# Two-layer YOCO trunk on one core: the first squares, the keys' low half, the last PLE product and the first weights are placed earlier, and ScalarE issues the transfers of layer one's key squares

## What is computed

```
q, k, v, z = split(x @ w_in_a, 4)                 # layer one: 2048 x 8192
z_scores = q k^T / sqrt(128);  past = key < query
log_1m = where(past, log_sigmoid(-z_scores), 0)
tail = reversed cumsum(log_1m) - log_1m
w = where(past, exp(log_sigmoid(z_scores) + tail), 0)
y = (w v  *  silu(z)) @ w_out_a
x = LayerNorm(alpha * x + y, ln_g, ln_b)
x = x + (p[i] @ w_ple[i]) * sigmoid(x @ w_ple_gate[i])
# shared K/V = split(LayerNorm(x) @ w_kv), K rotated; layer two:
q, z = split(x @ w_in_b, 2);  y = (softmax(rope(q) K^T) V * silu(z)) @ w_out_b
# then the same LayerNorm and the same PLE gate, whose result is the output
```

## Time and profile before

| | |
|---|---|
| median of 3 runs | 1149.44 us (1148.65 to 1149.66) |
| the profiled execution | 1152.77 us |
| its span, first to last instruction | 1151.1 us |
| busy: TensorE matmul, weight load | 1139.9 us (99%), 951.0 us (83%) |
| busy: VectorE, ScalarE, GpSimd | 745.8 us (65%), 590.9 us (51%), 232.6 us (20%) |
| chain that ended last, by engine | TensorE 91%, DMA 3%, VectorE, GpSimd, ScalarE, issue and SyncE 1% each |

### The profile page before, as it was taken

One profiled execution on the slowest core, in us unless ns is written; L12 is line 12 of the kernel. 1 busy time (PEld: TensorE's weight loads), 2 busy tenths in 40 slices (PEclk: granted clock), 3 DMA queues, 4 the chain that ended last, 5 costly groups with the idle time before them and its releaser, 6 DMA issues.

```text
span 1151.1 us, 15530 instructions
## 1 busy us (share of the span) xinstructions
PE 1139.9 (99%) x5274; PEld 951.0 (83%) x5274; DVE 745.8 (65%) x795; ACT 590.9 (51%) x669; POOL 232.6 (20%) x475
## 2 busy tenths in 40 slices
PE   9989999999999999999999999999999999999998
PEld 8878888888888888888888888888888888888887
DVE  6646556556465657578888785456776676656873
ACT  6555557446556453546454555555554545334641
POOL 1222320340232300002536753420000010000000
PEclk9999999999999999999999999999999999999999
DMA  9866775675676686457787876774555575763571
GB/s 305 270 208 178 208 217 151 195 228 171 185 209 178 199 311 217 148 164 256 228 275 228 246 243 215 226 218 149 183 161 183 159 243 162 258 199 117 190 239 70
DMA packets 126587, 235.67 MB, mean 205 GB/s; under 512 B 13856, under 2 KB 16160, under 8 KB 126032
## 3 DMA queue, kind: packets, MB, share of 16 engines
q1 hardware_dynamic: 110176, 209.74, 59.0%
q0 software_dynamic: 16368, 25.37, 6.8%
HBM read 216.71 MB, written 4.19 MB: 192 GB/s over the span
## 4 chain that ended last, share of the span: by engine, by line
PE 91%; DMA 3%; DVE 1%; POOL 1%; ACT 1%; issue 1%; SPq 1%; DVEq 0%; ACTq 0%
PE acc L1189 28%; PE acc L1191 28%; PE acc L1190 28%; DMA raw<-in_w_in_a 3%; PE aux L1223 2%; POOL heads L430 1%; PE aux L1216 1%; ACT w_hi L480 1%; DMA heads<-big 1%; PE aux L1249 1%; PE aux L1263 1%; DVE w_lo L749 1%; PE aux L1394 0%; PE aux L1238 0%; PE aux L1191 0%
## 5 line engine op out<-in xcount | busy, mean ns | idle before, releaser
L749 DVE TENSOR_TENSOR w_lo<-raw,w_hi 128x1024 fp32r<-128x1024 f32 x388 | 470.1, 1222 | 344.9 <-ACT w_hi L480 344.6
L480 ACT ACTIVATE w_hi<-raw 128x1024 fp32r<-128x1024 f32 x388 | 408.9, 1058 | 441.7 <-PE acc L1191 360.3
L1189 PE MATMUL acc<-w_hi,act 128*128 128x512 f32 x1548 | 608.0, 393 | 0.1
L1191 PE MATMUL acc<-w_hi,act 128*128 128x512 f32 x1548 | 603.1, 390 | 0.0
L1190 PE MATMUL acc<-w_lo,act 128*128 128x512 f32 x1548 | 602.6, 389 | 0.0
L1191 PEld LDWEIGHTS acc<-w_hi,act 128*128 128x128 f32 x1548 | 290.7, 188 | 61.4
L1189 PEld LDWEIGHTS acc<-w_hi,act 128*128 128x128 f32 x1548 | 290.9, 188 | 59.4 <-issue 0.7
L1190 PEld LDWEIGHTS acc<-w_lo,act 128*128 128x128 f32 x1548 | 291.0, 188 | 58.8
L430 POOL DMA_DIRECT2D heads<-big x192 | 93.8, 497 | 281.9 <-DVE big L770 238.1
L430 POOL DMA_DIRECT2D heads<-v_or_z x64 | 31.2, 496 | 52.0 <-DVE v_or_z L770 39.1
L430 POOL DMA_DIRECT2D stage<-v_or_z x48 | 23.5, 499 | 69.5 <-DVE v_or_z L988 43.7
(11 more groups left out here) (158 smaller groups left out, 653.2 us busy)
## 6 DMA issues: line engine op xcount, KB each, us to landing
raw<-in_w_in_a SPq DMA_DIRECT2D x124, 512.0 KB, 3.9
raw<-in_w_ple_gate SPq DMA_DIRECT2D x64, 512.0 KB, 4.8
raw<-in_w_in_b SPq DMA_DIRECT2D x64, 512.0 KB, 4.6
raw<-in_w_kv SPq DMA_DIRECT2D x64, 512.0 KB, 3.9
raw<-in_w_out_a SPq DMA_DIRECT2D x32, 512.0 KB, 4.5
raw<-in_w_out_b SPq DMA_DIRECT2D x32, 512.0 KB, 4.8
heads<-big POOLq DMA_DIRECT2D x192, 32.0 KB, 3.4
heads<-in_ln_rows POOLq DMA_DIRECT2D x4, 1024.0 KB, 7.9
```

What stands on the lines that cost most here:

```text
L480: nc.scalar.activation(w_hi[:, r], raw[:, r % RAWS], ACT.Copy).then_inc(hi_ready, 1)
L749: nc.vector.tensor_tensor(w_lo[:, r], raw[:, r % RAWS], w_hi[:, r].bitcast(F32), ALU.subtract) \
L1189: nc.tensor.matmul(dst, hi, w_hi[:, r, i], start=begin, stop=False)
L1191: mm = nc.tensor.matmul(dst, lo, w_hi[:, r, i], start=False, stop=end)
```

## The change

`WARM_UPS` is 12. The first two half pieces of weights are issued by ScalarE, ahead of its first instruction, and SyncE leaves them out. VectorE turns the first Q chunk after split 2 of its stretch (before: 3) and the first K chunk after split 3 (before: 6), ahead of `queries_lo(0)`. In all four groups `keys_lo` stands ahead of split 5. The key squares of all four groups are moved by 16 transfers that ScalarE issues after split 0 of the V chunk, with the same wait for `chunk_evac`; GpSimd keeps those of Q and Z. The tile 0 part of the last PLE product stands between the two token tiles of the last gate piece.

```
--- before.py
+++ after.py
@@ -34,7 +34,7 @@
 PIECE_K = 2
 RAWS = 4
 SPLITS = 8
-WARM_UPS = 14
+WARM_UPS = 12
 SQUARE = 32
 MOVED = 16 * (P // SQUARE) ** 2
 
@@ -335,7 +335,8 @@
                 for i, (x_sem, w_sem) in enumerate(((x_half_landed[j], w_half_landed[j]), (x_landed[j], w_landed[j]))):
                     rows = slice((j * PIECE_K + i) * P, (j * PIECE_K + i + 1) * P)
                     sp.dma_start(x_raw[:, PIECE_K * j + i], xt[rows, :]).then_inc(x_sem, 16)
-                    sp.dma_start(raw[:, j, i], wa[rows, 0:COLS]).then_inc(w_sem, 16)
+                    if j > 0:
+                        sp.dma_start(raw[:, j, i], wa[rows, 0:COLS]).then_inc(w_sem, 16)
             for j in range(RAWS, PC):
                 sp.dma_start(x_raw[:, PIECE_K * j:PIECE_K * (j + 1), :],
                              xt[j * PIECE_K * P:(j + 1) * PIECE_K * P, :].rearrange("(k p) t -> p k t", p=P)) \
@@ -433,7 +434,6 @@
 
             for g in range(G):
                 exchange(chunk_evac, g * 4 + 1, qT_flat, qn, q_moved)
-                exchange(chunk_evac, g * 4 + 2, kT_flat, kn, k_moved)
                 exchange(chunk_evac, g * 4 + 4, gt_flat, zn, z_moved)
             pool.wait_ge(pv_done, 2 * G)
             load_res(0, x)
@@ -586,6 +586,8 @@
                 nc.scalar.activation(w1_parts[:, 0, b], s[:, :, 0:T], ACT.Copy).then_inc(weights_hi, 1)
 
 
+            for i, w_sem in enumerate((w_half_landed[0], w_landed[0])):
+                act.dma_start(raw[:, 0, i], w_in_a[0][i * P:(i + 1) * P, 0:COLS]).then_inc(w_sem, 16)
             for j in range(RAWS):
                 for i, (x_sem, w_sem, x_done, w_done) in enumerate((
                         (x_half_landed[j], w_half_landed[j], x_half_hi, w_half_hi),
@@ -606,11 +608,23 @@
             nc.scalar.activation(neg_ones[:, :], neg_ones_raw, ACT.Copy).then_inc(masks_done, 1)
 
 
+            def exchange(turned, count, dst, src, moved):
+
+                act.wait_ge(turned, count)
+                for a in range(NS):
+                    for g in range(NS):
+                        act.dma_start(dst[g * SQUARE:(g + 1) * SQUARE, a * HT // NS:(a + 1) * HT // NS],
+                                      src[a * SQUARE:(a + 1) * SQUARE, g * HT // NS:(g + 1) * HT // NS]) \
+                            .then_inc(moved, 16)
+
+            def move_k(k):
+                exchange(chunk_evac, k * 4 + 2, kT_flat, kn, k_moved)
+
             def after_k(k):
                 return {5: [lambda: q_copies(k)]}
 
             def after_v(k):
-                return {4: [lambda: k_copies(k)], 6: [lambda: exp_abs(k, 0)],
+                return {0: [lambda: move_k(k)], 4: [lambda: k_copies(k)], 6: [lambda: exp_abs(k, 0)],
                         7: [lambda: values_hi(k), lambda: exp_abs(k, 1), lambda: log_1p(k)]}
 
             def after_z(k):
@@ -854,8 +868,7 @@
                 return {6: [lambda: queries_lo(k)]} | squares_end(n, 1, kn)
 
             def v_steps(k, n):
-                return {5: [lambda: keys_lo(k)],
-                        7: [lambda: values_lo(k), lambda: evacuate_v(n, 0, vn_a), lambda: softplus(k, 0)]}
+                return {7: [lambda: values_lo(k), lambda: evacuate_v(n, 0, vn_a), lambda: softplus(k, 0)]}
 
             def evacuate_v(n, parity, dst):
 
@@ -872,16 +885,16 @@
                 return {5: [lambda: gate_group(k, k, sz_a)], 6: [lambda: gated_lo(k, k, k + S_OUT[0])]}
 
             dve.wait_ge(consts_done, 12)
-            pieces(0, 0, {3: [lambda: turn_squares(PC, 0, qn)]})
-            pieces(PC, 0, {4: [lambda: queries_lo(0)], 6: [lambda: turn_squares(2 * PC, 1, kn)]})
+            pieces(0, 0, {2: [lambda: turn_squares(PC, 0, qn)]})
+            pieces(PC, 0, {3: [lambda: turn_squares(2 * PC, 1, kn)], 4: [lambda: queries_lo(0)]})
             with dve.Fori(0, G - 1) as g:
                 n = g * (4 * PC) + 2 * PC
-                pieces(n, 0, v_steps(g, n))
+                pieces(n, 0, v_steps(g, n), before={5: [lambda: keys_lo(g)]})
                 pieces(n + PC, 0, z_steps(g, n + PC))
                 pieces(n + 2 * PC, 0, gate_steps(g) | squares_end(n + 2 * PC, 0, qn))
                 pieces(n + 3 * PC, 0, k_steps(g + 1, n + 3 * PC))
             n = N_OUT[0] - 2 * PC
-            pieces(n, 0, v_steps(G - 1, n))
+            pieces(n, 0, v_steps(G - 1, n), before={5: [lambda: keys_lo(G - 1)]})
             pieces(n + PC, 0, z_steps(G - 1, n + PC))
 
             def add_residual(layer, c, used):
@@ -1171,7 +1184,7 @@
 
         @block.tensor
         def _(pe):
-            def piece(n, r, operand, tiles, out_banks, first, final, by_token=False, halves=False):
+            def piece(n, r, operand, tiles, out_banks, first, final, by_token=False, halves=False, between=None):
 
                 if halves:
                     pe.wait_ge(x_half_lo, n + 1)
@@ -1191,9 +1204,11 @@
                     mm = nc.tensor.matmul(dst, lo, w_hi[:, r, i], start=False, stop=end)
                     if by_token and t == 0 and end:
                         mm.then_inc(tile_0_done, 1)
+                        if between:
+                            between()
                 mm.then_inc(piece_used, 1)
 
-            def chunk(n, base, operand, parity, c, quarters=None, after=None, last=False):
+            def chunk(n, base, operand, parity, c, quarters=None, after=None, last=None):
 
                 if not isinstance(c, int) or c >= 2:
                     pe.wait_ge(chunk_evac, c - 1)
@@ -1205,7 +1220,7 @@
                     elif quarters is not None and j % 2 == 0:
                         pe.wait_ge(act_ready, quarters + j // 2 + 1)
                     piece(n + j, (base + j) % SPLITS, operand, range(PIECE_K * j, PIECE_K * (j + 1)),
-                          acc_of(parity), j == 0, j == PC - 1, by_token=last and j == PC - 1, halves=halves)
+                          acc_of(parity), j == 0, j == PC - 1, by_token=last and j == PC - 1, halves=halves, between=last)
                     for step in (after or {}).get(j, ()):
                         step()
 
@@ -1342,15 +1357,17 @@
                     chunk(c * PC + n, n, act0, c % 2, c + c0)
                 if layer:
                     c = G - 1
-                    chunk(c * PC + n, n, act0, c % 2, c + c0, last=True)
-                    last_ple_product()
-
-            def last_ple_product():
+                    chunk(c * PC + n, n, act0, c % 2, c + c0,
+                          last=lambda: last_ple_product(LAST_PARTS[0:1]))
+                    last_ple_product(LAST_PARTS[1:])
+
+            def last_ple_product(parts):
 
                 r = N_LAST % SPLITS
                 pe.wait_ge(lo_ready, N_LAST + 1)
                 pe.wait_ge(p_kept, 1)
-                for bank, (t, lo, hi) in enumerate(LAST_PARTS):
+                for t, lo, hi in parts:
+                    bank = LAST_PARTS.index((t, lo, hi))
                     for i in range(PIECE_K):
                         p_hi_t, p_lo_t = (p_last[:, s, i, t * P:(t + 1) * P] for s in range(2))
                         dst = aux_b[:, bank, lo:hi]
```

27 lines of the change are left out of this document (14 added, 13 removed).

## The result

| | before | after |
|---|---|---|
| median, us | 1149.38 (1148.65 to 1149.66, 4 runs) | 1156.24 (1155.93 to 1156.42, 4 runs) |
| the profiled execution's own time, us | 1152.77 | 1155.93 |
| its span, us | 1151.1 | 1154.2 |
| ratio after / before | | 1.006, 95% interval 1.0044 to 1.0075 |

The change makes the kernel slower by 6.9 us; forecast were 5.5 us less and a range that ended at 1147.5. The other sign came out, the one that the text gave a chance of 0.07.

The account below looks back on a forecast made before the run. TensorE, with work for 99% of the span, was taken as the bound, so only its waits could shrink. 1.9 + 1.4 + 1.6 + 0.6 = 5.5 us off the median 1149.44 gave 1143.9; 8-in-10 range 1140.8 to 1147.5.

Parts of the forecast that it names:

- The 16 issues on ScalarE: Key squares' transfers: 0.45 us each, 7.2 us in all, to 66.0; group one's scores at 72.0 against 73.91, gain 1.9 us.
- L: Length of ScalarE's 16 issues in a group, taken as 7.2 us; group one's scores then start at 64.8 + L.
- The start of the issues, 58.8: Group one: ScalarE issues only after split 24, which runs at 57.70 to 58.76, 1.5 us later than GpSimd did.
- rival A: Quick issues, 0.25 us or less, or issuing on during split 24; TensorE hardly waits: gain 8.6 us, 1140.8, chance 0.13.
- The splits behind the issues: Group one: four splits queue on ScalarE, 4.0 us to 70.0; copies done at 71.15, then keys_lo 0.1 and 0.68 us.
- Clock, 1.4 us: Group one's scores: TensorE idle 69.0 to 72.0, clock expected to stay up, 1.4 us gained; the other bound is 0.
- Groups two to four, 1.6 us: Key scores: keys_lo ready at 167.7, needed at 169.6, so 0.54 us of waiting goes in each of three groups.
- rival D: Slower: at 0.75 us an issue, late scores in all groups, 9.8 us more, 1159; decides from 0.6 us; chance 0.07.
- C: No difference: 0.57 us an issue leaves group one unchanged; to 0.65 groups two to four lose their gain; 1149.0, chance 0.09.
- Start, 0.5 without a term: Kernel start: fewer warm-ups and earlier weights bring the loads 0.5 us forward, not counted, since the keys' chain sets group one's end.
- End, 0.6: Last PLE product: its tile 0 part done early, so the last add ends at 1148.1 instead of 1148.71, 0.6 us.
- The descriptor generator: Shared by SyncE's and ScalarE's issues, by the skill's rule: sum would lose 0.7 us, or 2.1 if the clock falls.

Follow-up runs that it names:

- k_spread: The changed kernel with ScalarE's 16 key transfers issued in four lots of four, after splits 0, 1, 2 and 3 of the V chunk: 1149.46 us.
- k_sync_last: The changed kernel with the key moves back on GpSimd, except group four's sixteen, which SyncE issues: 1149.33 us.
- only_last_ple: The kernel before with one edit, the first part of the last PLE product computed between the last chunk's two token tiles: 1149.64 us.

## Why the prediction was wrong

- **The 16 issues on ScalarE: the step that failed.** It took 0.45 us an issue from SyncE's loads, the nearest rows. Measured 0.612, 0.64 apart: L is 10.3, not 7.2. SyncE's 0.59 for the same moves shows why: the rows used were of another transfer, and those of the earlier trace rows stand by themselves. The only ones in a row that the text had, SyncE's first, were 0.49 apart, above the 0.45 taken. The text saw the open question in the issuing engine; the engine made 0.02 us, the rest lay in what is issued and in issuing it in a row. Rows of the right transfer existed for GpSimd alone (0.496), and they were closer to the truth than the ones taken.
- **The start of the issues, 58.8, was wrong to the good.** They began at 56.65, during the table load in front of split 24, as rival A had it. This gave 2.15 us back.
- **The splits behind the issues.** ScalarE's 4.0 us were right (3.9). That VectorE's low halves of the same four take 0.19 us longer each was not seen. For it `keys_lo` starts 0.7 us behind the copies where 0.1 was forecast, 0.6 more. Together: 64.8 + 10.3 - 2.15 + 0.6 = 73.55; measured 73.57.
- **Clock, 1.4 us.** The argument was that an idle stretch short of 3.9 us leaves it up. It fell 1.7 to 2.7 us after the last matmul, so it could have fallen in the forecast's own idle stretch of 3.0 us (69.0 to 72.0) too. The term was not only 0 but -0.8, since it stayed low for longer than before. The other traces give no length of a wait from which it falls either: it fell within the 3.19 us of k_spread (0.57 in the stretch 72 to 73), but stood at 1.00 through and behind 3.17 us in k_sync_last (350 to 361) and 2.43 us in only_last_ple (68 to 80). The term could only have been given a chance.
- **Groups two to four, 1.6 us.** The sum given for rival D, 154.6 + L + 4.0 + 1.15 + 0.9, gives 170.9 with L = 10.3, and 171.5 with VectorE's 0.6; measured 171.62. TensorE could have begun at 170.04. Rival D was the case, a little above the 0.6 us from which it was said to decide. With the L measured, D's own steps give +1.2 in group one, 0.8 three times, -0.6: 3.0 us more, and the two spans differ by 3.1. That the sums meet is luck: group one came out at -0.3 and not +1.2, and the clock's 0.8 and 1.0 more in groups two to four (3.4, not 2.4), which D did not have, made up for it.
- **The chance of D.** It had 0.07, because it was priced at 0.75 us an issue only. The rows at hand ran from 0.37 to 0.60 for other transfers; that the price of this one lay inside or just above that range was likelier than that. C and D also overlap: C holds up to 0.65 us and gives no difference, D decides from 0.6 on. By D's own steps the gain of groups two to four is gone at 0.59 us an issue, and at 0.65 each of them is 0.9 us late, so C should have ended at 0.6 and D had its chance from there.
- **The base.** The gain in group one (1.9 + 1.4) was taken from a wait of 4.4 us with a clock fall behind it, and then subtracted from a median in which, by two further profiles, the wait is 1.4 to 2.4 us. Even with the forecast's own issue price, group one could give the median some 2.4 us at the most. Against the profiled execution the change loses 3.2 us, against the median 6.9: the other 3.7 are this.
- **Start, 0.5 without a term.** 0.2 measured in the last matmul of the V chunk's piece 6 (68.95 against 69.15). The wait for the second half is gone, but the first product starts 0.16 us later (6.48 against 6.32).
- **End, 0.6.** Right in the trace, 0.64; alone it is too small to show in the median (only_last_ple).
- **GpSimd and the earlier Q squares, nothing.** Right; no wait in the K chunk.
- **The descriptor generator.** ScalarE's issues in group one lay between 0.609 and 0.627 us, though SyncE issued two loads in that time, which took 0.373 us each (0.372 without ScalarE's issues), and the same moves took 0.59 on SyncE alone. The rule of the Trainium skill (Perfetto Trace Analysis, DMA Instruction — HWDGE), by which the two would delay each other, is neither needed for the loss nor seen in it; two loads are few to judge it by.

## What to carry to other kernels

Price a DMA issue by a row of the same transfer, issued in a row as it will be, not by one on the same kind of queue; where there is none, let the range reach above the slowest row. When an engine that also computes is given issues, follow what piles up behind them on this engine, then on the next one, then on the queue whose buffers it frees. Before a term is taken from a stall in the trace, compare that execution's own time with the median: a stall that only a slow execution has cannot be won from the median.

The cheapest edit won here: one low half written ahead of a split instead of behind it gave 4.0 us; of the edits beside it, none gave anything that the measurement could tell.

## What had not been expected of the hardware

- An issue of a 32 x 256 move inside SBUF takes 0.61 us on ScalarE's queue and 0.59 on SyncE's, longer than on GpSimd's (0.496) and longer than SyncE's own loads of 512 KB (0.372 by themselves, 0.467 in a row). ScalarE's two first weights, 128 x 512 from HBM, took 0.90 us together. What in the smaller transfer makes it dearer stays open; fewer moves of more rows each were not tried.
- ScalarE's queue issues while the engine is busy: the first two issues run during the table load in front of split 24, the next two start before that split ends at 58.86. Only the work placed behind the issues waits for them.
- Of the waits of one to five us at group one's scores, the same code showed 1.4, 2.4 and 4.4 us in three executions.
